# Gate projection of the last block: two products for each k tile instead of three, with a ScalarE copy and a VectorE add

## The chip, the cores and the metric

The kernel runs on one core of one Trainium2 chip. The metric is device time in microseconds (us), the median of several runs. Lower is better.

## The reference

The model is two blocks of mixers with expert layers, and then a last block. Only the last block is touched. For its 256 rows `x` of width 1024 it computes `z = rmsnorm(x) @ w_in`, and splits `z` into `a_in`, `a_gate`, `q`, `k`, `v`, `b_gp` and `g_logits`. The change is in the product that gives three of these:

```
y_a = (multiscale_pool(a_in) * silu(a_gate)) @ w_proj_a
y_b = (dilated_attention(q, k, v) * silu(b_gp)) @ w_proj_b
gates = sigmoid(g_logits + b_gate)            # 2 x 1024 columns
x = x + (gates[0] * y_a + gates[1] * y_b) @ w_out
```

`a_gate` and `b_gp` have 512 columns each and `g_logits` has 2048, so the "gates" stage multiplies 256 rows of width 1024 by 3072 columns. All of it is float32.

## The kernel before

**How a product is made exact enough.** A float32 operand is held as two fp32r parts: a high part (a copy) and a low part (the rest). A product is high by high, plus high by low, plus low by high. The rows are in `XH` and `XL`. They are the two halves of one tile, `X2[:, k, :, :]`, so that 512 adjacent elements are the high and the low part of one k tile of 128. Weights come from HBM in chunks of 128x1024. ScalarE makes `WH` (`high`, L159), then VectorE (`low_v`, L164) or GpSimd (`low_g`, L169, the odd chunks of this stage) makes `WL = raw - WH`. Four slots (`NW`) hold chunks in turn, and `w_used` counts chunks that TensorE has finished.

**The stage.** The gates have 24 chunks. A pair of chunks (`kh` 0 and 1, each with four k tiles) makes two column blocks `j` of 128. The output lies transposed: 128 weight columns on the partitions, 256 rows along the free axis. Weights are the stationary operand, rows are the moving one. `chunk_T` (L190) issues for each k tile and block the three products of `three` (L175 to L178), 256 columns each, into `PS[:, bank, 0:256]`; a chunk has 24. Pairs use banks 0 and 1, then 2 and 3, by turns. After the second chunk of a pair, ScalarE empties bank `j = 0` and VectorE bank `j = 1` (L2119, L2121, L2232, L2234); from pair 8 on ScalarE empties both and applies the sigmoid on the way (L2126). The remaining eight sigmoids run late, from SBUF (L2143).

**What is woven in.** Attention runs in the same loop. After each chunk `c` up to 15, `att2_tensor(t, c + 2)` issues, in this order, the weighted sum of step `i - 2` (L1949, 12 products), the six transposes of step `i - 1` (L1957) and, up to step 15, the scores of step `i` (L1971). Here `i = c + 2`. The scores wait for `b_o`, because they overwrite the banks from which VectorE reads the weighted sum:

```
if i >= 2:
    t.wait_ge(b_o, i - 1)
```

`b_o` is raised in `att2_vector(v, i)` by the scaling of the weighted sum of step `i - 2` (L2171). On VectorE the order within one turn of the loop is: low part of a coming chunk (even `c` only), emptying of the gates (odd `c` only), then `att2_vector(c + 2)`: scaling (L2171), reciprocal (L2176), scores plus bias (L2186), maximum (L2190). On ScalarE it is: high part of a coming chunk (L159), emptying of the gates (odd `c`), then `att2_scalar(c + 2)`: copy of the transposed weights (L2081), exponential (L2085). Each engine runs its instructions in the order written.

**What follows.** After the gates come four chunks of `w_proj_a` (PA) and four of `w_proj_b` (PB), all with `chunk_T` and three products, and then the output projection. On ScalarE the copies of branch b (L2147) stand right behind the last gates. On VectorE the matching subtractions (L2257), the low part of the third PA chunk (L164) and the merge of the first PA chunk (L2274) follow in that order.

`two` (L180 to L183) was there already: the expert layers and their query projection use it. It issues one product of 512 columns (high weights by both parts of the rows) and one of 256 (low weights by the high rows). The expert layers then copy the second half of the bank to `BESIDE` (L1009) on ScalarE and add it on VectorE (L1233).

Of the kernel before, what the change touches and what calls it, by code (L numbers as in the profile page):

```python
# [7 lines left out]
ALU = mybir.AluOpType  # L8
ACT = mybir.ActivationFunctionType
# [8 lines left out]
NW = 4  # L18
# [53 lines left out]
def build(nc, d, out):  # L72
    ctx = ExitStack()
    with ctx:
# [3 lines left out]
        def sem(name):  # L78
            return ctx.enter_context(nc.semaphore(name))
# [3 lines left out]
        XH, XL = X2[:, :, 0, :], X2[:, :, 1, :]  # L83
        raw = sb("raw", [128, NW, SLOT])
        WH = sb("WH", [128, NW, SLOT], F32R)
# [18 lines left out]
        PVT = sb("pvt", [128, PV_N])  # L104
# [66 lines left out]
        def wait_low(e, i):  # L171
            e.wait_ge(w_low_g if low_on_g[i] else w_low_v, low_count[i])
# [7 lines left out]
        def two(t, bank, w, k, first, last):  # L180

            t.matmul(PS[:, bank, :], w[0], X2[:, k, :, :].rearrange("p w t -> p (w t)"), start=first, stop=False)  # L182
            return t.matmul(PS[:, bank, 0:256], w[1], X2[:, k, 0, :], start=False, stop=last)  # L183
# [1656 lines left out]
        def mixer1_gpsimd(g):  # L1840
# [57 lines left out]
        q2_up, k2_up, v2_a, v2_v = sem("q2_up"), sem("k2_up"), sem("v2_by_scalar"), sem("v2_by_vector")  # L1898
        b_mm, b_s, b_mx, b_e, b_T, b_pt, b_r, b_w, b_o = (sem(n) for n in (
            "b_scores", "b_biased", "b_max", "b_exp", "b_turned", "b_pt", "b_inverse", "b_weighed", "b_out"))  # L1900
        gr_a, gr_v, gs_up, sw_up, mx_up, bg_T, bg_up = (sem(n) for n in (
            "gates_by_scalar", "gates_by_vector", "gates_sigmoid", "branches_silu", "branch_a_up", "att_turned2",
            "branch_b_up"))

        y_h, y_l, mg_a, mg_b = sem("merge_high"), sem("merge_low"), sem("merge_a"), sem("merge_b")
# [69 lines left out]
        def block2_tensor(t):  # L1975
# [48 lines left out]
            def gate_bank(pair, j):  # L2024
                if pair < 2:
                    t.wait_ge(v2_v if j else v2_a, 2 + pair)
                elif pair < 10:
                    t.wait_ge(gr_v if j else gr_a, pair - 1)
                else:
                    t.wait_ge(gs_up, 2 * (pair - 10) + j + 1)  # L2030
            for c in range(24):
                pair, kh = divmod(c, 2)
                chunk_T(t, G0 + c, [PS[:, 2 * (pair % 2) + j, 0:256] for j in range(2)], (XH, XL), kh, 8, None,
                        lambda j: gate_bank(pair, j))
                if c < 16:
                    att2_tensor(t, c + 2)
                if c == 17:
                    t.wait_ge(b_o, 16)
                    t.wait_ge(b_pt, 16)
                    for n in range(2):  # L2040
                        for j in range(2):
                            for tt in range(2):
                                m = t.transpose(PS[:, 4 + n, j * 256 + tt * 128:j * 256 + tt * 128 + 128],
                                                ATT[:, tt, (2 * n + j) * 128:(2 * n + j) * 128 + 128], ident)
                        m.then_inc(bg_T, 1)

            def pa_bank(pair, j):
                if pair < 2:
                    t.wait_ge(gs_up, 5 + 2 * pair + j)
                else:  # L2050
                    t.wait_ge(mg_a, 2 * (pair - 2) + j + 1)
            for pair in range(4):
# [22 lines left out]
        def att2_scalar(a, i):  # L2075
# [6 lines left out]
            if i < 16:  # L2082
                s_ = SB[i % 3]
                a.wait_ge(b_mx, i + 1)
                a.activation(s_, s_, ACT.Exp, bias=MXB[:, i:i + 1], accum_out=SUB[:, i:i + 1]).then_inc(b_e, 1)  # L2085

        def block2_scalar(a):
            norm_scalar(a, 4, XS2, lambda t, h: x_after_up(a, 3, t, h))
            split_scalar(a, 4, PV_MIX2)
            for c in range(4):  # L2090
                high(a, A0 + c + 3)
            a.wait_ge(w_used, A0 + 4)
            a.activation(AI[:, 0, :], PS[:, 0, :], ACT.Copy).then_inc(ai_a, 1)
            for c in range(24):
                high(a, QK0 + c + 3)
                if c % 2 and c >= 12:
                    pair = c // 2
                    a.wait_ge(w_used, QK0 + c + 1)
                    for j in range(2):
                        a.activation(KT2[:, 2 * pair + j - 12, :], PS[:, 2 * ((pair + 1) % 2) + j, 0:256],  # L2100
                                     ACT.Copy).then_inc(k2_up, 1)
            for c in range(12):
                high(a, V0 + c + 3)
                if c % 4 == 3:
                    nb = c // 4
                    a.wait_ge(w_used, V0 + c + 1)
                    a.activation(VN[:, 0, nb * 512:nb * 512 + 512], PS[:, 2 * ((nb + 1) % 2), :], ACT.Copy).then_inc(v2_a, 1)
                if c in (8, 9):
                    att2_scalar(a, c - 8)
            for c in range(24):  # L2110
                high(a, G0 + c + 3)
                if c % 2:
                    pair = c // 2
                    blk = 2 * pair
                    a.wait_ge(w_used, G0 + c + 1)
                    if pair < 8:
                        ps = PS[:, 2 * (pair % 2), 0:256]
                        if blk < 8:
                            a.activation((SAG if blk < 4 else BGT)[:, blk % 4, :], ps, ACT.Copy).then_inc(gr_a, 1)  # L2119
                        else:  # L2120
                            a.activation(GT[:, blk - 8, :], ps, ACT.Identity,  # L2121
                                         bias=PVT[:, PV_BG + blk - 8:PV_BG + blk - 7]).then_inc(gr_a, 1)
                    else:
                        for j in range(2):
                            b = blk + j
                            a.activation(GT[:, b - 8, :], PS[:, 2 * (pair % 2) + j, 0:256], ACT.Sigmoid,  # L2126
                                         bias=PVT[:, PV_BG + b - 8:PV_BG + b - 7]).then_inc(gs_up, 1)
                if c < 16:
                    att2_scalar(a, c + 2)
                if c == 16:  # L2130
                    a.wait_ge(gr_a, 4)
                    a.wait_ge(gr_v, 4)
                    a.activation(AR[:, 10240:12288], AR[:, 10240:12288], ACT.Silu).then_inc(sw_up, 1)
                if c == 18:
                    a.wait_ge(mx_up, 1)
                    for n in range(2):
                        a.activation(YH[:, 2 * n:2 * n + 2, :], MIX[:, 2 * n:2 * n + 2, :], ACT.Copy).then_inc(y_h, 1)
                if 18 <= c < 22:
                    for j in range(2):
                        b = 2 * (c - 18) + j  # L2140
                        a.wait_ge(gr_v, 8)
                        a.wait_ge(gr_a, 8)
                        a.activation(GT[:, b, :], GT[:, b, :], ACT.Sigmoid).then_inc(gt_sig, 1)  # L2143
            for n in range(2):
                a.wait_ge(bg_up, n + 1)
                a.wait_ge(w_used, PA0)
                a.activation(XH[:, 4 + 2 * n:6 + 2 * n, :], BGT[:, 2 * n:2 * n + 2, :], ACT.Copy).then_inc(y_h, 1)  # L2147

            def merged(kp):
                a.wait_ge(mg_b, 2 * kp + 2)  # L2150
                a.wait_ge(w_used, PA0 if kp < 2 else W0)
                a.activation(XH[:, 2 * kp:2 * kp + 2, :], MG[:, 2 * kp:2 * kp + 2, :], ACT.Copy).then_inc(y_h, 1)
            for c in range(8):
                high(a, PA0 + c + 3)
                if c in (4, 5):
                    merged(c - 4)
            for kp in (2, 3):
                merged(kp)
            table(a, ACT.Sqrt)
            for c in range(8):  # L2160
                high(a, W0 + c + 3)
            norm_scalar(a, 5, SQ2, lambda t, h: x_after_out(a, 4, t, h))


        def att2_vector(v, i):
# [11 lines left out]
            if i < 16:  # L2177
# [11 lines left out]
                v.wait_ge(b_s, i + 1)  # L2189
                v.tensor_reduce(MXB[:, i:i + 1], s_, AX, ALU.max, negate=True).then_inc(b_mx, 1)  # L2190

        def block2_vector(v):
            norm_vector(v, 4, XS2)
            split_vector(v, 4, PV_MIX2)
# [28 lines left out]
                    att2_vector(v, c - 8)  # L2223
            for c in range(24):
                low_v(v, G0 + c + 2)
                if c % 2 and c < 16:
                    pair = c // 2
                    blk = 2 * pair + 1
                    v.wait_ge(w_used, G0 + c + 1)
                    ps = PS[:, 2 * (pair % 2) + 1, 0:256]  # L2230
                    if blk < 8:
                        v.tensor_copy((SAG if blk < 4 else BGT)[:, blk % 4, :], ps).then_inc(gr_v, 1)  # L2232
                    else:
                        v.tensor_scalar(GT[:, blk - 8, :], ps, PVT[:, PV_BG + blk - 8:PV_BG + blk - 7], None,  # L2234
                                        ALU.add).then_inc(gr_v, 1)
                if c < 16:
                    att2_vector(v, c + 2)
                if c == 16:
# [25 lines left out]
            for c in range(8):  # L2264
                low_v(v, PA0 + c + 2)
                v.wait_ge(w_used, PA0 + c + 1)
                if c == 0:
                    v.wait_ge(gs_up, 8)
                    v.wait_ge(gt_sig, 8)
                for j in range(2):  # L2270
                    blk = 2 * (c % 4) + j
# [176 lines left out]
```

## Time and profile before

| | before |
|---|---|
| median of 3 runs | 2162.6 us (2161.62 to 2164.62) |
| the profiled execution's own time | 2162.53 us |
| its span | 2160.7 us |
| TensorE busy (matmul) | 2125.7 us, 98% |
| VectorE busy | 1460.7 us, 68% |
| ScalarE busy | 1270.8 us, 59% |
| GpSimd busy | 357.8 us, 17% |

The profile gives the start of an instruction in us from the start of the span, and how long it took. The gates stage lies at about 1983 to 2107 us. TensorE is the engine that has least idle time; in a row of the weights' load (PEld) or the product (PE) the engine's next instruction may start before the shown end of the one before, since ends of products are modelled. So distances between starts are the ones to measure with.

### The profile page before, as it was taken

The numbers are of one execution on the slowest core, as the hardware profiler recorded it, in microseconds if no ns is written. First come the engines' busy times: TensorE is split into PE (matmuls) and PEld (weight loads), VectorE is DVE, ScalarE is ACT, GpSimd is POOL, SyncE is SP. The second block draws the span as 40 slices with busy tenths as digits, with TensorE's granted clock in tenths as the row PEclk, the third lists the DMA queues.
The fourth block names the chain that finished last, engine by engine and source line by source line (L and its number), as shares of the span: only waits on it lengthen the run. The fifth ranks groups of instructions, "written<-read, shape, count | busy, mean of one in ns | idle before, by whom it ended". The sixth has DMA issues, their size and how long they took to land.

```text
span 2160.7 us, 32784 instructions
## 1 busy us (share of the span) xinstructions
PE 2125.7 (98%) x12752; PEld 1855.5 (86%) x12752; DVE 1460.7 (68%) x2546; ACT 1270.8 (59%) x2137; POOL 357.8 (17%) x171
## 2 busy tenths in 40 slices
PE   8899999999999999999999999999999999999998
PEld 7789988888888888887899888888888888898997
DVE  7658988889855555557489888898555555423445
ACT  6664588877644444455545888876444444444464
POOL 1437800000000000011378000000000000243131
PEclk9999999999999999999999999999999999999999
DMA  6445655555566666653456555555666666754244
GB/s 220 143 132 166 186 170 164 174 169 170 159 205 195 193 193 191 195 178 113 126 165 184 174 167 168 174 173 163 203 194 194 194 192 192 254 185 147 80 136 127
DMA packets 104893, 373.19 MB, mean 173 GB/s; under 512 B 12140, under 2 KB 15620, under 8 KB 104356
## 3 DMA queue, kind: packets, MB, share of 16 engines
q1 hardware_dynamic: 104740, 371.11, 55.8%
q8 instruction: 101, 1.65, 0.3%
q14 instruction: 52, 0.43, 0.1%
HBM read 369.97 MB, written 1.10 MB: 172 GB/s over the span
## 4 chain that ended last, share of the span: by engine, by line
PE 93%; DVE 3%; ACT 2%; DMA 1%; issue 1%; POOL 0%; SPq 0%; ACTq 0%; POOLq 0%; DVEq 0%
PE ps L182 20%; PE ps L176 18%; PE ps L178 18%; PE ps L177 18%; PE ps L183 10%; PE ps L907 3%; PE ps L1971 1%; PE ps L1949 1%; DMA raw<-in_w_qk_dram 1%; DVE WL L164 1%; PE ps L277 1%; PE ps L886 1%; PE ps L1957 1%; PE ps L1422 0%; PE ps L287 0%
## 5 line engine op out<-in xcount | busy, mean ns | idle before, releaser
L159 ACT ACTIVATE WH<-raw 128x1024 fp32r<-128x1024 f32 x680 | 717.6, 1057 | 506.8 <-PE ps L178 457.1
L164 DVE TENSOR_TENSOR WL<-raw,WH 128x1024 fp32r<-128x1024 f32 x556 | 680.3, 1225 | 104.3 <-ACT WH L159 104.1
L182 PE MATMUL ps<-X,WH 128*128 128x512 f32 x1888 | 669.0, 398 | 0.1
L183 PE MATMUL ps<-X,WL 128*128 128x256 f32 x1888 | 527.8, 280 | 0.0
L169 POOL TENSOR_TENSOR WL<-raw,WH 128x1024 fp32r<-128x1024 f32 x124 | 307.6, 2483 | 1001.5 <-ACT WH L159 1000.6
L182 PEld LDWEIGHTS ps<-X,WH 128*128 128x128 f32 x1888 | 353.9, 187 | 79.1 <-issue 0.5
L176 PE MATMUL ps<-WH,X 128*128 128x512 f32 x960 | 378.3, 394 | 6.7 <-DVE X L1607 3.4
L178 PE MATMUL ps<-WH,X 128*128 128x512 f32 x960 | 374.5, 390 | 0.0
L177 PE MATMUL ps<-WL,X 128*128 128x512 f32 x960 | 374.3, 390 | 0.0
L183 PEld LDWEIGHTS ps<-X,WL 128*128 128x128 f32 x1888 | 356.4, 189 | 0.0
L176 PE MATMUL ps<-X,WH 128*128 128x256 f32 x896 | 256.2, 286 | 1.0 <-DVE WL L164 1.0
L177 PE MATMUL ps<-X,WH 128*128 128x256 f32 x896 | 253.5, 283 | 0.0
L178 PE MATMUL ps<-X,WL 128*128 128x256 f32 x896 | 253.5, 283 | 0.0
L176 PEld LDWEIGHTS ps<-WH,X 128*128 128x128 f32 x960 | 180.7, 188 | 47.1 <-DVE X L1607 4.1
L178 PEld LDWEIGHTS ps<-WH,X 128*128 128x128 f32 x960 | 180.6, 188 | 38.1
L177 PEld LDWEIGHTS ps<-WL,X 128*128 128x128 f32 x960 | 180.8, 188 | 37.1 <-issue 0.5
L176 PEld LDWEIGHTS ps<-X,WH 128*128 128x128 f32 x896 | 171.7, 192 | 6.3 <-issue 2.7
L177 PEld LDWEIGHTS ps<-X,WH 128*128 128x128 f32 x896 | 171.9, 192 | 0.1
L178 PEld LDWEIGHTS ps<-X,WL 128*128 128x128 f32 x896 | 171.8, 192 | 0.0
L991 ACT ACTIVATE ONE<-ONE,GATE 128x128 f16<-128x128 f16 x512 | 167.6, 429 | 0.0
L1252 DVE TENSOR_TENSOR X<-arena,X 128x512 fp32r<-128x512 f32 x84 | 58.1, 692 | 161.9 <-ACT X L1038 161.9
L177 PE MATMUL ps<-WL,GH 128*128 128x512 f32 x352 | 137.0, 389 | 0.0
(300 smaller groups left out, 2356.5 us busy)
## 6 DMA issues: line engine op xcount, KB each, us to landing
raw<-in_l_down_dram SPq DMA_DIRECT2D x256, 512.0 KB, 3.6
raw<-in_l_up_dram SPq DMA_DIRECT2D x256, 512.0 KB, 4.3
raw<-in_l_wq_dram SPq DMA_DIRECT2D x32, 512.0 KB, 3.6
raw<-in_w_qk_dram SPq DMA_DIRECT2D x24, 512.0 KB, 3.8
raw<-in_w_gates_dram SPq DMA_DIRECT2D x24, 512.0 KB, 3.6
raw<-in_l_nat_dram SPq DMA_DIRECT2D x16, 512.0 KB, 3.6
raw<-in_l_wout_dram SPq DMA_DIRECT2D x16, 512.0 KB, 3.6
raw<-in_l_win_dram SPq DMA_DIRECT2D x16, 512.0 KB, 4.1
```

What stands on the lines that cost most here:

```text
L159: a.activation(WH[:, i % NW, :], raw[:, i % NW, :], ACT.Copy).then_inc(w_high, 1)
L164: v.tensor_tensor(WL[:, i % NW, :], raw[:, i % NW, :], WH[:, i % NW, :], ALU.subtract).then_inc(w_low_v, 1)
L169: g.tensor_tensor(WL[:, i % NW, :], raw[:, i % NW, :], WH[:, i % NW, :], ALU.subtract).then_inc(w_low_g, 1)
L176: t.matmul(o, a[0], b[0], start=first, stop=False)
L177: t.matmul(o, a[0], b[1], start=False, stop=False)
L178: return t.matmul(o, a[1], b[0], start=False, stop=last)
L182: t.matmul(PS[:, bank, :], w[0], X2[:, k, :, :].rearrange("p w t -> p (w t)"), start=first, stop=False)
L183: return t.matmul(PS[:, bank, 0:256], w[1], X2[:, k, 0, :], start=False, stop=last)
L277: t.matmul(PS[:, bank, 384:512], ident, ident, start=True, stop=True)
L907: m = t.matmul(PS[:, 6 + j // 4, (j % 4) * 128:(j % 4) * 128 + 128], ONE[:, s % 2, 0, g, :, tt], ROWS[:, s % 2, 1 + k, g, :, tt], start=(k ...
L991: a.activation(ROWS[:, s % 2, 1, g, :, t], ROWS[:, s % 2, 2, g, :, t], ACT.Copy, scale=GATE0[:, 8 * s + j:8 * s + j + 1]).then_inc(row_0, 1)
L1252: v.tensor_tensor(gl, G[:, 2 * p:2 * p + 2, :].rearrange("p e t -> p (e t)"), gh, ALU.subtract).then_inc(g_low, 1)
```

## The change

The 24 gate chunks use `two` in place of `three`: per k tile and block one product of 512 columns and one of 256. The bank then holds two halves that must be added. ScalarE copies the second halves of both banks of a pair to `BESIDE` (128x512 in one instruction), for all twelve pairs. VectorE waits for this copy and adds: one `tensor_tensor` of 128x512 for pairs 0 to 3, and two `scalar_tensor_tensor` of 128x256 with the bias for pairs 4 to 11. ScalarE no longer applies the sigmoid out of PSUM: all sixteen gate blocks get it late, in eight activations of 128x512 from SBUF. The semaphore `gs_up` is gone; `gr_a` now counts copies and `gr_v` pairs.

```diff
             for c in range(24):
                 pair, kh = divmod(c, 2)
-                chunk_T(t, G0 + c, [PS[:, 2 * (pair % 2) + j, 0:256] for j in range(2)], (XH, XL), kh, 8, None,
-                        lambda j: gate_bank(pair, j))
+                wait_low(t, G0 + c)
+                for j in range(2):
+                    if kh == 0:
+                        gate_bank(pair, j)
+                    for kk in range(4):
+                        m = two(t, 2 * (pair % 2) + j,
+                                [v[:, (G0 + c) % NW, kk * 256 + j * 128:kk * 256 + j * 128 + 128] for v in (WH, WL)],
+                                4 * kh + kk, kh + kk == 0, kh == 1 and kk == 3)
+                m.then_inc(w_used, 1)
...
+        def gates_sigmoid(a, n):
+            a.wait_ge(gr_v, 5 + n)
+            a.activation(GT[:, 2 * n:2 * n + 2, :], GT[:, 2 * n:2 * n + 2, :], ACT.Sigmoid).then_inc(gt_sig, 1)
...
                 if c % 2:
                     pair = c // 2
-                    blk = 2 * pair
+                    b = 2 * (pair % 2)
                     a.wait_ge(w_used, G0 + c + 1)
...
+                    if pair >= 2:
+                        a.wait_ge(gr_v, pair - 1)
+                    a.activation(BESIDE[:, pair % 2], PS[:, b:b + 2, 256:512], ACT.Copy).then_inc(gr_a, 1)
+                if c >= 18:
+                    gates_sigmoid(a, c - 18)
...
+            for n in (6, 7):
+                gates_sigmoid(a, n)
...
+        def gates_vector(v, pair):
+
+            blk, b = 2 * pair, 2 * (pair % 2)
+            v.wait_ge(gr_a, pair + 1)
+            if pair < 4:
+                o = (SAG if blk < 4 else BGT)[:, blk % 4:blk % 4 + 2, :]
+                v.tensor_tensor(o, PS[:, b:b + 2, 0:256], BESIDE[:, pair % 2], ALU.add).then_inc(gr_v, 1)
+            else:
+                for j in range(2):
+                    n = blk + j - 8
+                    m = v.scalar_tensor_tensor(out=GT[:, n, :], in0=PS[:, b + j, 0:256], scalar=PVT[:, PV_BG + n:PV_BG + n + 1],
+                                               in1=BESIDE[:, pair % 2, j], op0=ALU.add, op1=ALU.add)
+                m.then_inc(gr_v, 1)
...
-                if c % 2 and c < 16:
...
+                if c % 2:
+                    gates_vector(v, c // 2)
                 if c < 16:
                     att2_vector(v, c + 2)
```

## Rows read from the trace of the kernel before

**Rows 1.** The page: TensorE's busy time (share, count), and the chain that ended last.
```profile
PE 2125.7 (98%) x12752; PEld 1855.5 (86%) x12752; DVE 1460.7 (68%) x2546; ACT 1270.8 (59%) x2137; POOL 357.8 (17%) x171
...
PE 93%; DVE 3%; ACT 2%; DMA 1%; issue 1%; POOL 0%; SPq 0%; ACTq 0%; POOLq 0%; DVEq 0%
```
**Rows 2.** Busy time by stage: PE, PEld, DVE, ACT, POOL, then granted clock, DMA share, GB/s.
```profile
1983.00:2107.00 124.00, 124.00 (x951) 115.39 (x950) 57.30 (x88) 63.35 (x95) 31.45 (x13) 1.00 0.35 108
```
**Rows 3.** TensorE in order of time (start, us, what): gate chunks 16, 17, 48 products between.
```profile
2083.10 0.36 PE L176 MATMUL ps<-X,WH 128*128 128x256 f32 x1
...
2088.94 0.82 PE L2043 MATMUL ps<-cst,arena 128*128 128x128 f32 x6
```
**Rows 4.** TensorE in order of time: two chunk pairs of the query projection, 32 products each.
```profile
153.86 0.47 PE L182 MATMUL ps<-X,WH 128*128 128x512 f32 x1
...
159.50 1.05 PE L886 MATMUL ps<-arena 128*128 128x128 f32 x8
...
166.75 0.48 PE L182 MATMUL ps<-X,WH 128*128 128x512 f32 x1
...
172.49 1.05 PE L886 MATMUL ps<-arena 128*128 128x128 f32 x8
```
**Rows 5.** TensorE in order of time: gate chunk 3 and the attention step behind it.
```profile
2002.39 0.39 PE L176 MATMUL ps<-X,WH 128*128 128x256 f32 x1
...
2005.37 1.45 PE L1949 MATMUL ps<-arena 128*128 128x64 f32 x12
2006.66 0.83 PE L1957 MATMUL ps<-cst,arena 128*128 128x128 f32 x6
2007.42 1.56 PE L1971 MATMUL ps<-arena 64*128 64x256 f32 x6
```
**Rows 6.** ScalarE in order of time, the same turn of the loop.
```profile
2005.41 1.04 ACT L159 ACTIVATE WH<-raw 128x1024 fp32r<-128x1024 f32 x1
2006.36 0.36 ACT L2119 ACTIVATE arena<-ps 128x256 f32<-128x256 f32 x1
```
**Rows 7.** VectorE in order of time, the same turn of the loop.
```profile
2005.57 0.42 DVE L2232 COPY arena<-ps 128x256 f32<-128x256 f32 x1 [1.13 <-PE ps L178]
2006.86 0.28 DVE L2171 TENSOR_SCALAR arena<-ps,sm 128x64 f32<-128x64 f32 x1 [0.86 <-PE ps L1949]
```
**Rows 8.** ScalarE in the first expert layer: the copy of a second half.
```profile
278.11 0.60 ACT L1009 ACTIVATE BESIDE<-ps 128x512 f32<-128x512 f32 x1 [0.50 <-PE ps L183]
```
**Rows 9.** VectorE there: the add behind this copy, and its next instruction.
```profile
278.74 0.69 DVE L1233 TENSOR_TENSOR arena<-ps,BESIDE 128x512 f32<-128x512 f32 x1 [1.08 <-ACT BESIDE L1009]
279.35 0.68 DVE L1219 TENSOR_TENSOR ONE<-ONE,GP 128x1024 f16<-128x1024 f16 x1
```
**Rows 10.** Groups of instructions, VectorE, 1840 to 1870 us (busy us, mean ns | idle before).
```profile
L306 DVE SCALAR_TENSOR_TENSOR X<-ps,pvt,X 128x256 fp32r<-128x256 f32 x8 | 3.2, 476 | 1.7 <-ACT X L298 1.7
```
**Rows 11.** The chain that ended last, in order of time: VectorE releases TensorE.
```profile
1870.20 1.24 DVE WL L164
1871.48 0.38 PE ps L176
```
**Rows 12.** TensorE in order of time: starts of the first and the third PA chunk.
```profile
2107.08 0.28 PE L176 MATMUL ps<-Y,WH 128*128 128x256 f32 x1
...
2112.84 0.28 PE L176 MATMUL ps<-Y,WH 128*128 128x256 f32 x1
```
**Rows 13.** ScalarE behind the last gates.
```profile
2108.01 1.15 ACT L2147 ACTIVATE X<-arena 128x512 fp32r<-128x512 f32 x2
```
**Rows 14.** VectorE behind the last gates.
```profile
2109.88 1.22 DVE L164 TENSOR_TENSOR WL<-raw,WH 128x1024 fp32r<-128x1024 f32 x1
2111.02 0.75 DVE L2274 TENSOR_TENSOR arena<-ps,arena 128x256 f32<-128x256 f32 x2
```
**Rows 15.** VectorE beside GpSimd, in order of time: two views, one row of each.
```profile
2091.91 2.90 DVE L2253 TENSOR_TENSOR Y<-arena,Y 128x512 fp32r<-128x512 f32 x1
...
2091.00 3.26 POOL L169 TENSOR_TENSOR WL<-raw,WH 128x1024 fp32r<-128x1024 f32 x1 [3.98 <-ACT WH L159]
```

More of the change, by code:

```diff
@@ L1900, in build @@
             "b_scores", "b_biased", "b_max", "b_exp", "b_turned", "b_pt", "b_inverse", "b_weighed", "b_out"))
-        gr_a, gr_v, gs_up, sw_up, mx_up, bg_T, bg_up = (sem(n) for n in (
-            "gates_by_scalar", "gates_by_vector", "gates_sigmoid", "branches_silu", "branch_a_up", "att_turned2",
+        gr_a, gr_v, sw_up, mx_up, bg_T, bg_up = (sem(n) for n in (
+            "gates_by_scalar", "gates_by_vector", "branches_silu", "branch_a_up", "att_turned2",
             "branch_b_up"))
@@ L2026, in gate_bank @@
                     t.wait_ge(v2_v if j else v2_a, 2 + pair)
-                elif pair < 10:
-                    t.wait_ge(gr_v if j else gr_a, pair - 1)
                 else:
-                    t.wait_ge(gs_up, 2 * (pair - 10) + j + 1)
+                    t.wait_ge(gr_v, pair - 1)
             for c in range(24):
                 pair, kh = divmod(c, 2)
-                chunk_T(t, G0 + c, [PS[:, 2 * (pair % 2) + j, 0:256] for j in range(2)], (XH, XL), kh, 8, None,
-                        lambda j: gate_bank(pair, j))
+                wait_low(t, G0 + c)
[7 more added lines that the diff above has]
+                m.then_inc(w_used, 1)
                 if c < 16:
@@ L2048, in pa_bank @@
                 if pair < 2:
-                    t.wait_ge(gs_up, 5 + 2 * pair + j)
+                    t.wait_ge(gr_v, 11 + pair)
                 else:
@@ L2113, in block2_scalar @@
                     pair = c // 2
-                    blk = 2 * pair
+                    b = 2 * (pair % 2)
                     a.wait_ge(w_used, G0 + c + 1)
[L2116 to L2127, printed above, removed]
+                    if pair >= 2:
[3 more added lines that the diff above has]
+                    gates_sigmoid(a, c - 18)
                 if c < 16:
@@ L2130, in block2_scalar @@
                 if c == 16:
-                    a.wait_ge(gr_a, 4)
                     a.wait_ge(gr_v, 4)
@@ L2137, in block2_scalar @@
                         a.activation(YH[:, 2 * n:2 * n + 2, :], MIX[:, 2 * n:2 * n + 2, :], ACT.Copy).then_inc(y_h, 1)
[L2138 to L2143, printed above, removed]
+            for n in (6, 7):
+                gates_sigmoid(a, n)
             for n in range(2):
@@ L2225, in block2_vector @@
                 low_v(v, G0 + c + 2)
-                if c % 2 and c < 16:
[L2227 to L2235, printed above, removed]
+                if c % 2:
+                    gates_vector(v, c // 2)
                 if c < 16:
@@ L2267, in block2_vector @@
                 if c == 0:
-                    v.wait_ge(gs_up, 8)
                     v.wait_ge(gt_sig, 8)
```

## The prediction

> **What bounds the kernel now.** I read the page first: TensorE is busy 98% of the span and carries 93% of the chain that ended last [rows 1]. Busy time by stage comes next. Over the gates, 1983 to 2107 us, TensorE is busy all of the 124.00 us at a granted clock of 1.00, while VectorE works 57.30 us and ScalarE 63.35 us [rows 2]. So a product less on TensorE is worth its whole distance between starts, and work added to the other two costs nothing until it makes TensorE wait. The question for each added instruction is therefore which TensorE wait it stands in front of. Within the stage I read the three engines in order of time over one turn of the loop [rows 5 to 7].
>
> **TensorE's gain.** Per k tile and block, three products of 256 columns become one of 512 and one of 256. The columns streamed are the same, 768. What goes is one instruction and one weight load. The two forms can be compared in the trace, with the same operands in the same roles. With three, the 48 products of two chunks take 2088.94 - 2083.10 = 5.84 us [rows 3]. With two, a pair of chunks in the query projection has 32 products; four of the seven full pairs there take 159.50 - 153.86 = 5.64 us and three take 172.49 - 166.75 = 5.74 us [rows 4]. Their mean is 5.68 us, 0.16 less for two chunks. Most gate chunks stand alone between attention steps, which costs 2005.37 - 2002.39 = 2.98 us for one [rows 5], slightly more than half of 5.84. I take 0.09 us per chunk, so 24 x 0.09 = 2.2 us. The bounds are 12 x 0.10 = 1.2 us (all pairs like the slower row) and 12 x 0.20 = 2.4 us (all like the faster). At 24 chunks x 8 x one instruction, 2.2 us are 11 ns for each instruction removed.
>
> The rows put the 48 products at 0.12 us a start [rows 3]. Against this the Trainium skill (TensorE: Matmul & The Clock Gate, section "Wait — 56ns, not 53.3ns?") says that back-to-back warm products start N / 2.4 GHz + about 2.5 ns apart. By that rule 256 columns would be 109 ns, the removed instruction would be worth 2.5 ns, and the whole gain 192 x 2.5 ns = 0.5 us. The trace does not agree for this operand type, since 5.84 us / 48 is 122 ns. I go by the rows.
>
> **The wait that it adds.** The scores of a step (L1971) wait for VectorE's scaling of the weighted sum (L2171), which stands behind the emptying of the gates in VectorE's order. Before, this was harmless. VectorE's copy starts 0.20 us after the chunk, at 2005.57, and it is idle again before the scaling at 2006.86 [rows 7]. That scaling ends at 2007.14, and the scores start at 2007.42, behind the transposes [rows 5].
>
> After the change VectorE must first wait for ScalarE's copy, and ScalarE is late. It runs the exponential and then the high part of a weight chunk, and gets to the gates only at 2006.36 [rows 6], 0.99 us after the chunk's end. This time does not hang on the chunk's end but on what came before it (scores, maximum, exponential), so it stays 2006.36 - 2002.39 = 3.97 us after the chunk's start. I work in that time:
>
> - ScalarE's copy starts at 3.97.
> - VectorE's add starts 278.74 - 278.11 = 0.63 later [rows 8, 9], at 4.60.
> - The next VectorE instruction starts 279.35 - 278.74 = 0.61 behind the add [rows 9]. So the scaling starts at 5.21 and ends 0.28 later [rows 7], at 5.49.
> - VectorE to TensorE takes 1871.48 - (1870.20 + 1.24) = 0.04 [rows 11], so the scores may start at 5.53.
> - Without the wait they would start at (2.98 - 0.09) + (2007.42 - 2005.37) = 2.89 + 2.05 = 4.94 [rows 5].
>
> TensorE waits 0.59, say 0.6 us. With the biased form (pairs 4 and later) VectorE has two instructions in place of the add. Eight of this kind are busy 3.2 us together, 0.40 us each [rows 10], so 0.80 in place of 0.61, and the wait is 0.8 us. The stop happens at odd chunks that are followed by scores, which are c = 1, 3, 5, 7 (add) and 9, 11, 13 (biased). After c = 15 there are no scores. The sum is 4 x 0.6 + 3 x 0.8 = 4.8 us. At even chunks nothing is emptied and nothing changes. The delay doesn't grow from turn to turn, since scores, maximum and exponential all start later with TensorE.
>
> Bounds of the 4.8: if the last products' end and not the high part let ScalarE begin, its copy would start at the chunk's end + 0.20, all would be ready 0.20 + 0.63 + 0.61 + 0.28 + 0.04 = 1.76 after the chunk, ahead of 2.05, and the loss would be 0. From above: let no instruction overlap the end of the one before, which puts the add at 0.69 [rows 9] and the two biased ones at 2 x 0.476 = 0.95 [rows 10], and let the release take 0.20, as from the chunk's end to VectorE's copy [rows 5, 7], in place of 0.04. That adds 4 x 0.24 + 3 x 0.31 = 1.9 us, 6.7 in all. The rows are nearest to the middle, because every link of the sum has one.
>
> **Late gates, sigmoids.** Without attention ScalarE and VectorE have a whole pair (about 5.7 us) to empty two banks, and need 0.63 + 0.80. ScalarE's work falls there: sixteen activations out of PSUM and eight late sigmoids of 256 go, and twelve copies and eight sigmoids of 512 come. I cost it at nothing until the last pair.
>
> Behind the last pair ScalarE before had its two sigmoids and began the branch copies at 2108.01, 0.93 us after the first PA product at 2107.08 [rows 12, 13]. Now it has a copy at 0.20, then three sigmoids. The two branch copies of the same size took 1.15 for two [rows 13], with an end overlap of about 0.08 that leaves some 0.53 each. So the branch copies begin at 0.20 + 0.49 + 3 x 0.53 = 2.28, which is 1.35 us later. VectorE's subtractions, the low part of PA's third chunk and the first merge all move by 1.35. The first of the two merges freed its bank at about 2111.02 + 0.42 = 2111.44, and TensorE needed it at 2112.84 [rows 12, 14]: a slack of 1.4 us. The low part was ready at 2111.10, a slack of 1.7. So the slack is just used up. I take 0.1 us, with bounds 0 and 0.5. Behind it everything is again counted from TensorE.
>
> **The sum.** -2.2 + 4.8 + 0.1 = +2.7 us. The profiled execution's own time is 2162.53 us (span 2160.7 and 1.8 around it), as good as the median of 2162.6. The forecast is 2165.2 us. A difference of 0.2%, 4.3 us, is about what a measurement here can tell from no change; the forecast is inside it, on the slow side.
>
> **Rivals.**
>
> - *The wait never binds (faster).* TensorE gets its 2.2 us and the stops are 0: 2162.5 - 2.2 + 0.1 = 2160.4 us. For it: VectorE has 0.86 us of idle before the scaling [rows 7]. Against it: ScalarE's place in the order. It decides at the start of the copy. If it came before 4.94 - 0.63 - 0.61 - 0.28 - 0.04 = 3.38 us after the chunk's start, there would be no stop; the row has 3.97.
> - *Columns alone set the pace.* Then 768 columns take as long in either form, the gain is 0, and the time is 2162.5 + 4.8 + 0.1 = 2167.4 us. Against it is the comparison of [rows 3, 4], though those lie 1900 us apart. The rule of the Trainium skill named above comes near to this: with 0.5 us of gain it would be 2166.9.
> - *VectorE meets GpSimd behind the last gates.* A VectorE subtraction of two SBUF operands took 2.90 us when GpSimd's was already running [rows 15], against the 0.6 us of its like. If GpSimd's next low part begins ahead of VectorE's, the third PA chunk comes some 2.3 us late: 2167.5 us. For it: VectorE's work moves by 1.35 us. Against it: ScalarE's high part, which releases GpSimd, stands behind the same branch copies and moves with it. The Trainium skill (SBUF — State Buffer, section "Who interferes with whom") calls it an exclusive lock for the whole instruction; the row agrees. The new adds read one operand from PSUM, so they don't take part.
> - *Each stop is longer.* With the upper bound of 6.7 us the time is 2162.5 - 2.2 + 6.7 + 0.1 = 2167.1, and with the smaller gain of 1.2 us 2168.1 us.
>
> **Chances.** Forecast 0.70, no wait 0.10, columns alone 0.06, the meeting with GpSimd 0.06, longer stops 0.08. The first two lie within 0.2% of before, except for a few hundredths at the edges. Of the other three (0.20) most lie past 2166.9. So faster 0.02, same 0.81, slower 0.17. The likeliest case's own range is 2163.5 to 2166.6. The full range reaches 2161.5 (stops half as long, and scatter of the runs) to 2168.0.
>
> **What would show it.** A pair of gate chunks 16 and 17 takes about 5.65 us. Between L1957 and L1971 TensorE waits at seven odd chunks, 0.6 us at four and 0.8 us at three, released by VectorE's L2171 line; at even chunks it doesn't. VectorE's idle before the new adds is released by ScalarE's copy, which starts about 3.97 us after the chunk. A turn of the loop becomes 0.09 us shorter at even chunks and 0.5 to 0.7 us longer at odd ones. The forecast is wrong if these waits are missing, if a chunk is not shorter, or if the third PA chunk starts more than 0.5 us late.

## The result and the profile after

The changed kernel takes 2165.68 us (median of 20 runs, 2164.05 to 2167.69) against 2163.37 us before (20 runs, 2161.34 to 2165.07). The ratio of the two is 1.0013, with a 95% interval of 1.0007 to 1.0019. It is 2.3 us slower by the medians, where +2.7 us was forecast. The interval excludes 1, and the difference is inside the 0.2% that the prediction called no change.

The spans of the two profiled executions differ by only 2162.2 - 2160.7 = 1.5 us. The code ahead of the gates is the same in both, and yet the first gate product starts at 1981.48 us instead of 1982.98. That is scatter of earlier stages, so I compare the distance between two events of one trace: the first gate product and the first product of the next projection (PA). I call it the stage. It was 124.10 us before. Here are the stage and the PA chunks in the changed kernel (columns as in [rows 2]), and then TensorE's waits within the stage (who waited for whom, us in total, times, longest).

```profile
1981.48:2108.39 126.91, 123.00 (x760) 105.16 (x759) 60.22 (x98) 64.13 (x89) 31.25 (x13) 1.00 0.35 105
2108.39:2120.05 11.66, 11.66 (x99) 11.56 (x97) 7.40 (x12) 7.24 (x10) 6.51 (x2) 1.00 0.54 165
```

```profile
PE ps L1971 <- DVE arena L2168: 3.9, 7, 0.7
```

The stage is 2.81 us longer. TensorE, which was busy all of it in [rows 2], now stands idle for 126.91 - 123.00 = 3.9 us. All of that is one wait, seven times: the scores (L1971) for VectorE's scaling (L2168, which was L2171). (A stop costs slightly more than the idle time shown for it, 0.54 us against 0.48 in the turn below, since the shown end of the transposes lies past the point at which the scores would have started.) The granted clock is still 1.00. PA is 0.14 us longer than before, where its row was:

```profile
2107.08:2118.60 11.52, 11.52 (x99) 11.52 (x97) 5.74 (x10) 6.01 (x8) 6.14 (x2) 1.00 0.63 181
```

The three engines in gate chunk 3, the turn of [rows 5 to 7], look like this. First TensorE, in order of time:

```profile
2001.28 0.50 PE L182 MATMUL ps<-X,WH 128*128 128x512 f32 x1
...
2004.21 1.45 PE L1949 MATMUL ps<-arena 128*128 128x64 f32 x12
2005.49 0.82 PE L1957 MATMUL ps<-cst,arena 128*128 128x128 f32 x6
2006.79 1.56 PE L1971 MATMUL ps<-arena 64*128 64x256 f32 x6 [0.48 <-DVE arena L2168]
```

Then ScalarE:

```profile
2004.30 1.04 ACT L159 ACTIVATE WH<-raw 128x1024 fp32r<-128x1024 f32 x1
2005.25 0.57 ACT L2127 ACTIVATE BESIDE<-ps 128x512 f32<-128x512 f32 x1
2006.35 0.81 ACT L2086 ACTIVATE arena<-ps 128x768 f32<-128x768 f32 x1 [0.53 <-PE ps L1957]
```

And VectorE:

```profile
2005.85 0.69 DVE L2195 TENSOR_TENSOR arena<-ps,BESIDE 128x512 f32<-128x512 f32 x1 [2.52 <-ACT BESIDE L2127]
2006.46 0.28 DVE L2168 TENSOR_SCALAR arena<-ps,sm 128x64 f32<-128x64 f32 x1
```

Read them as one chain, counted from the chunk's start at 2001.28. ScalarE runs the high part of a weight chunk until about then, and its copy starts at 3.97. The add starts at 4.57, the scaling at 5.18 and ends at 5.46, and the scores start at 5.51. The transposes would have let them start at 2.93 + 2.04 = 4.97, so the stop is 0.54 us. With the biased form (pairs 4 and later) VectorE does two instructions before the scaling:

```profile
2046.19 0.88 DVE L2199 SCALAR_TENSOR_TENSOR arena<-ps,pvt,BESIDE 128x256 f32<-128x256 f32 x2 [2.52 <-ACT BESIDE L2127]
2046.98 0.28 DVE L2168 TENSOR_SCALAR arena<-ps,sm 128x64 f32<-128x64 f32 x1
```

```profile
2047.31 1.56 PE L1971 MATMUL ps<-arena 64*128 64x256 f32 x6 [0.65 <-DVE arena L2168]
```

Here, in chunk 9, the scaling starts 0.79 us behind the first of them instead of 0.61. The scores start 2.76 us after that chunk's end at 2044.55, against 2.03 to 2.04 at the turns without a stop.

### The profile page after: what moved, and what is told of

The parts are those of the page before. It is cut to its first block, busy times and chain, and to the rows that moved or that the text cites. A ratio compares the mean times of both kernels' runs of the same rounds, so it can differ in the third digit from the quotient of the medians.

```text
span 2162.2 us, 32409 instructions
## 1 busy us (share of the span) xinstructions
PE 2124.5 (98%) x12560; PEld 1845.5 (85%) x12560; DVE 1465.3 (68%) x2558; ACT 1272.5 (59%) x2133; POOL 357.9 (17%) x171
## 4 chain that ended last, share of the span: by engine, by line
PE 92%; DVE 4%; ACT 2%; issue 2%; POOL 0%; DMA 0%; SPq 0%; ACTq 0%; DVEq 0%; POOLq 0%
PE ps L182 22%; PE ps L176 17%; PE ps L178 17%; PE ps L177 17%; PE ps L183 11%; PE ps L907 3%; PE ps L1971 1%; PE ps L277 1%; DVE WL L164 1%; PE ps L886 1%; PE ps L1949 1%; PE ps L287 0%; PE ps L1422 0%; DVE arena L2183 0%; DVE sm L2187 0%
## 5 line engine op out<-in xcount | busy, mean ns | idle before, releaser
L182 PE MATMUL ps<-X,WH 128*128 128x512 f32 x2080 | 739.1, 398 | 0.1
L182 PEld LDWEIGHTS ps<-X,WH 128*128 128x128 f32 x2080 | 390.0, 187 | 91.8 <-issue 5.1
L183 PEld LDWEIGHTS ps<-X,WL 128*128 128x128 f32 x2080 | 392.7, 189 | 0.0
L176 PE MATMUL ps<-X,WH 128*128 128x256 f32 x704 | 200.1, 284 | 0.0
L177 PE MATMUL ps<-X,WH 128*128 128x256 f32 x704 | 199.2, 283 | 0.0
L178 PE MATMUL ps<-WH,GL 128*128 128x512 f32 x352 | 136.9, 389 | 0.0
L176 PE MATMUL ps<-WH,GH 128*128 128x512 f32 x352 | 136.9, 389 | 0.0
L176 PEld LDWEIGHTS ps<-X,WH 128*128 128x128 f32 x704 | 135.1, 192 | 0.2
```

The costliest lines, as they stand in the source:

```text
L176: t.matmul(o, a[0], b[0], start=first, stop=False)
L177: t.matmul(o, a[0], b[1], start=False, stop=False)
L178: return t.matmul(o, a[1], b[0], start=False, stop=last)
```

## The experiments

All times are compared with the kernel before, run on the same chip. For a few tenths of a us the stage in the trace is the sharper measure, since the times of one kernel spread over 3 us or more. By the times alone e1, e2 and e4 are at the edge of no change (their intervals reach 1.0), so what is said of these three rests on the stage.

**e1_scale_first.** Only VectorE's order changes: the scaling goes in front of the add.

```diff
-        def att2_vector(v, i):
+        def att2_vector(v, i, between=None):
...
                 v.reciprocal(SUB[:, n:n + 1], SUB[:, n:n + 1]).then_inc(b_r, 1)
+            if between is not None:
+                gates_vector(v, between)
...
-                if c % 2:
+                if c % 2 and c >= 16:
                     gates_vector(v, c // 2)
                 if c < 16:
-                    att2_vector(v, c + 2)
+                    att2_vector(v, c + 2, c // 2 if c % 2 else None)
```

> The changed kernel with one thing reordered on VectorE: at odd chunks up to 15 the scaling of the weighted sum (and the reciprocal) comes first, then the add of the two gate halves, then scores plus bias and maximum. Work and products are the same. Theory (the scores wait for a scaling that stands behind an add that stands behind a late ScalarE copy): the waits of L1971 on VectorE, 0.53 us at four and 0.72 us at three odd chunks (4.3 us in all), vanish. The stage from the first gate product to the first PA product, 124.10 us before and 126.91 us after, becomes 122.6 us, and the time is about 1.4 us under the kernel before (near 2162.0, ratio 0.9993). Rival A (more VectorE and ScalarE work in the stage slows it wherever it stands): stage near 126.9, ratio 1.0013. Rival B (the add now delays scores plus bias): a new wait before the exponential, each odd turn 0.2 us or more too long, stage 124 to 126.

Measured: 2161.81 us (11 runs), ratio 0.9991 (0.9982 to 1.0). The stage, the same turn on VectorE, and the same on TensorE:

```profile
1981.86:2104.14 122.28, 122.28 (x759) 105.00 (x758) 61.62 (x98) 64.15 (x89) 30.26 (x13) 1.00 0.35 109
```

```profile
2005.51 0.28 DVE L2168 TENSOR_SCALAR arena<-ps,sm 128x64 f32<-128x64 f32 x1 [2.36 <-PE ps L1949]
2005.71 0.15 DVE L2173 RECIPROCAL sm<-sm 128x1 f32<-128x1 f32 x1
2005.78 0.67 DVE L2197 TENSOR_TENSOR arena<-ps,BESIDE 128x512 f32<-128x512 f32 x1
```

```profile
2004.03 1.45 PE L1949 MATMUL ps<-arena 128*128 128x64 f32 x12
2005.31 0.82 PE L1957 MATMUL ps<-cst,arena 128*128 128x128 f32 x6
2006.06 1.56 PE L1971 MATMUL ps<-arena 64*128 64x256 f32 x6
```

The scores start 2.03 us after the chunk, and TensorE is busy for all of the 122.28 us. With the same work on every engine the stage is 4.63 us shorter than in the changed kernel. The seven turns with a stop, each from chunk start to chunk start, account for 49.59 - 45.17 = 4.42 us of this. The other 0.2 us are not stops. The largest part lies in the last six chunks, where TensorE waits in neither kernel; here they are in the changed kernel and then in e1:

```profile
2091.34:2108.39 17.05, 17.05 (x100) 14.81 (x99) 9.69 (x13) 12.15 (x17) 7.91 (x3) 1.00 0.53 170
```

```profile
2087.42:2104.14 16.72, 16.72 (x99) 14.63 (x98) 9.71 (x13) 12.16 (x17) 7.93 (x3) 1.00 0.62 196
```

These 0.33 us are taken up again at the end; in the remaining chunks the difference is 0.1 us the other way.

Rival A (more work slows it wherever it stands) and rival B (the add delays what follows) both fall.

**e2_copy_first.** Only ScalarE's order changes, at odd chunks up to 15; VectorE still scales behind the add.

```diff
-                high(a, G0 + c + 3)
+                if c % 2 == 0 or c >= 16:
+                    high(a, G0 + c + 3)
...
                     a.activation(BESIDE[:, pair % 2], PS[:, b:b + 2, 256:512], ACT.Copy).then_inc(gr_a, 1)
+                    if c < 16:
+                        high(a, G0 + c + 3)
```

> The changed kernel with one thing reordered on ScalarE: at odd chunks up to 15 the copy of the second halves comes ahead of the high part of a weight chunk. VectorE's order is that of the changed kernel. Theory: ScalarE's copy starts 0.20 us after the chunk instead of 1.04, the scaling is done 1.8 to 1.95 us after the chunk and the scores could start at 2.05 anyway, so the stops vanish here too although the scaling still stands behind the add: stage 122.6 us, about 1.4 us under the kernel before. Rival A (the place of the scaling behind the add is what costs, whenever the copy comes): stops stay at 0.5 to 0.7 us, stage 126.9. Rival B (the high part, now 0.5 us later, makes a weight chunk late): a wait of TensorE for a low part, not for L2168.

Measured: 2162.11 us (11 runs), ratio 0.9991 (0.9982 to 1.0). The stage, and then TensorE, ScalarE and VectorE in the same turn:

```profile
1983.34:2105.62 122.28, 122.28 (x759) 105.01 (x758) 60.40 (x98) 64.93 (x89) 30.37 (x13) 1.00 0.36 109
```

```profile
2002.58 0.50 PE L182 MATMUL ps<-X,WH 128*128 128x512 f32 x1
...
2005.51 1.45 PE L1949 MATMUL ps<-arena 128*128 128x64 f32 x12
2006.79 0.82 PE L1957 MATMUL ps<-cst,arena 128*128 128x128 f32 x6
2007.54 1.13 PE L1971 MATMUL ps<-arena 64*128 64x256 f32 x4
```

```profile
2005.70 0.60 ACT L2128 ACTIVATE BESIDE<-ps 128x512 f32<-128x512 f32 x1
2006.20 1.05 ACT L159 ACTIVATE WH<-raw 128x1024 fp32r<-128x1024 f32 x1
```

```profile
2006.34 0.69 DVE L2198 TENSOR_TENSOR arena<-ps,BESIDE 128x512 f32<-128x512 f32 x1 [1.70 <-ACT BESIDE L2128]
2006.99 0.28 DVE L2171 TENSOR_SCALAR arena<-ps,sm 128x64 f32<-128x64 f32 x1
```

The copy starts 0.19 us after the chunk, the scaling is done at 1.76, and the scores start at 2007.54, which is 2.03. So the scaling may stand behind the add, as long as the copy comes in time. It took both to make the stop: a consumer behind the add on VectorE, and the copy behind the high part on ScalarE. Taking away either removes all of it.

**e3_three_products.** The changed kernel with three products of 256 columns, into the two halves of the bank.

```diff
+        def split3(t, bank, w, k, first, last):
+
+            t.matmul(PS[:, bank, 0:256], w[0], X2[:, k, 0, :], start=first, stop=False)
+            t.matmul(PS[:, bank, 256:512], w[0], X2[:, k, 1, :], start=False, stop=False)
+            return t.matmul(PS[:, bank, 0:256], w[1], X2[:, k, 0, :], start=False, stop=last)
...
-                        m = two(t, 2 * (pair % 2) + j,
+                        m = split3(t, 2 * (pair % 2) + j,
```

> The changed kernel with three products of 256 columns again, of which high weights by low rows goes into the second half of the bank; copy, adds, sigmoids and all orders as in the changed kernel. It shows what one instruction less is worth while everything else stays. Theory: even chunks and those from 15 on lengthen by 0.063 us each; at the seven odd chunks with a stop a longer chunk costs nothing, since the copy counts from the chunk's start, so their stops shrink from 0.53 to 0.48 and from 0.72 to 0.67. Stage 126.91 + 17 x 0.063 = 128.0 us, time about 3.9 us over the kernel before (ratio 1.0018). Rival (columns alone set the pace, and the stage gained nothing from fewer products): stage 126.9, as after.

Measured: 2168.21 us (11 runs), ratio 1.0024 (1.0015 to 1.0033). The stage, and TensorE's waits in it:

```profile
1985.48:2113.54 128.06, 124.57 (x951) 115.46 (x950) 60.22 (x98) 64.14 (x89) 31.30 (x13) 1.00 0.34 104
```

```profile
PE ps L1977 <- DVE arena L2174: 3.5, 7, 0.6
```

The stage is 1.15 us longer than in the changed kernel (expected 1.1), and the stops total 3.5 us instead of 3.9. Fewer products do pay, but where there is a stop the shorter chunk only makes the stop longer.

**e4_products_only.** The kernel before with the two products and its own emptying. The half of the bank with high weights by low rows isn't added, so that product is missing from the gates.

```diff
-                chunk_T(t, G0 + c, [PS[:, 2 * (pair % 2) + j, 0:256] for j in range(2)], (XH, XL), kh, 8, None,
-                        lambda j: gate_bank(pair, j))
+                wait_low(t, G0 + c)
+                for j in range(2):
+                    if kh == 0:
+                        gate_bank(pair, j)
+                    for kk in range(4):
+                        m = two(t, 2 * (pair % 2) + j,
...
+                m.then_inc(w_used, 1)
```

> The kernel before with the products of the change alone: one of 512 columns and one of 256 for each k tile, and the emptying of before (0:256 of each bank, ScalarE and VectorE in parallel, sigmoids out of PSUM). The second half of each bank is left out, so the product of high weights and low rows is missing from the gates. Theory: no stop, 24 chunks of 0.063 us less, stage 124.10 - 1.5 = 122.6 us, time 1.5 us under the kernel before (ratio 0.9993). Rival (columns alone): stage 124.1, ratio 1.0. Rival (my sizing before the result, 0.09 us per chunk): stage 121.9.

Measured: 2162.25 us (11 runs), ratio 0.9991 (0.9982 to 1.0).

```profile
1982.56:2104.95 122.39, 122.39 (x760) 105.19 (x759) 57.36 (x88) 63.38 (x95) 31.41 (x13) 1.00 0.36 109
```

The products alone gain 124.10 - 122.39 = 1.71 us, as good as e1's 1.82. So with the order of e1, the copy and the add cost nothing in the stage. The rival of columns alone falls. 1.8 us over 24 chunks are 0.076 us each; expected were 0.063 (from the result) and 0.09 (from the prediction).

**e6_one_add.** The changed kernel, biased pairs with one add as well. It leaves out the bias of the gates.

```diff
-                for j in range(2):
-                    n = blk + j - 8
-                    m = v.scalar_tensor_tensor(out=GT[:, n, :], in0=PS[:, b + j, 0:256], scalar=PVT[:, PV_BG + n:PV_BG + n + 1],
-                                               in1=BESIDE[:, pair % 2, j], op0=ALU.add, op1=ALU.add)
-                m.then_inc(gr_v, 1)
+                v.tensor_tensor(GT[:, blk - 8:blk - 6, :], PS[:, b:b + 2, 0:256], BESIDE[:, pair % 2],
+                                ALU.add).then_inc(gr_v, 1)
```

> The changed kernel, with the two biased instructions of pairs 4 to 11 replaced by one add of 128x512, as in pairs 0 to 3. The bias of the gates is left out. Theory (a stop is the sum of the links copy, add, scaling): the three stops at c = 9, 11, 13 shrink from 0.72 to 0.53 us, which is the 0.19 us between 0.80 and 0.61; the other four stay. Stage 126.91 - 0.57 = 126.3 us, time 0.6 us under the changed kernel, 1.7 over the kernel before (ratio 1.0008). Rival (the longer stops at later pairs come from something else that changes there): stops stay at 0.72, stage 126.9.

Measured: 2166.1 us (10 runs), ratio 1.0012 (1.0003 to 1.0022), which can't be told from the changed kernel. The stage, and the scores behind chunk 11, which starts at 2056.01 and ends at 2058.89:

```profile
1982.33:2108.87 126.54, 122.95 (x759) 105.18 (x758) 59.09 (x91) 64.09 (x89) 30.80 (x13) 1.00 0.35 106
```

```profile
2061.52 0.70 PE L1971 MATMUL ps<-arena 64*128 64x256 f32 x2 [0.52 <-DVE arena L2168]
```

The scores start 5.51 us after the chunk's start, the same as in pair 1 of the changed kernel, so the chain is what I said. The turns of c = 9, 11 and 13, from chunk start to chunk start, fall from 7.19, 7.20 and 7.19 us to 7.00, which is the 0.57 us expected. The stage nevertheless shrinks by only 0.37 us. The missing 0.20 us is in turns without a stop: the chunks c = 6, 12 and 14 take 2.94 us each here and 2.89, 2.88 and 2.88 in the changed kernel. Why they differ wasn't tried. Counted from the chunk's end the stop at c = 11 is 2.63 - 2.04 = 0.59 us and not the 0.53 expected, because this chunk took only 2.88 us; I had treated the chunk as constant.

**e7_branch_first.** The kernel of e1 with the last three sigmoids behind the branch copies.

```diff
-                if c >= 18:
+                if 18 <= c < 23:
                     gates_sigmoid(a, c - 18)
...
-            for n in (6, 7):
-                gates_sigmoid(a, n)
...
+            for n in (5, 6, 7):
+                gates_sigmoid(a, n)
```

> The kernel of e1_scale_first with ScalarE's last three sigmoids behind the two branch copies instead of ahead of them. In the kernel before, PA (first PA product to first PB product) takes 11.52 us; in the changed one 11.66, since the first merge of PA frees its bank 5.7 us after the last gate and TensorE wants it at 5.76. Theory: the branch copies begin 1.6 us earlier, PA is back at 11.52 us, stage of the gates 122.3 as in e1; 0.15 us in all, which the times can't show. Rival (the 0.14 us comes from GpSimd's subtraction beside VectorE's, not from the sigmoids): PA stays at 11.66.

Measured: 2161.73 us (10 runs), ratio 0.9989 (0.998 to 0.9999). PA in e1 and then in e7:

```profile
2104.14:2115.81 11.67, 11.67 (x99) 11.56 (x97) 7.41 (x12) 7.23 (x10) 6.53 (x2) 1.00 0.51 160
```

```profile
2104.90:2116.41 11.51, 11.51 (x99) 11.51 (x98) 6.59 (x12) 7.22 (x10) 5.44 (x2) 1.00 0.63 194
```

PA is back at the 11.5 us of the kernel before, so the 0.14 us of the changed kernel came from the place of the sigmoids. They are lost where the third PA chunk begins: in e1 two starts in a row are 0.21 and 0.19 us apart there instead of 0.12 (2109.77, 2109.98, 2110.17). That chunk needs the bank which the first merge frees, but the profile shows no wait there, so this last link is argued and not shown. VectorE's low part that is slow beside GpSimd starts only at 2110.76, so it isn't the cause. As a time it can't be seen.

**e5_qk_too.** The kernel of e1, with the 24 chunks of the q and k projection changed in the same way. The core of it:

```diff
-                chunk_T(t, QK0 + c, [PS[:, 2 * ((pair + 1) % 2) + j, 0:256] for j in range(2)], (XH, XL), kh, 8, None,
-                        lambda j: qk_bank(pair, j))
...
+                        m = two(t, 2 * ((pair + 1) % 2) + j,
...
+                    a.activation(BESIDE[:, pair % 2], PS[:, b:b + 2, 256:512], ACT.Copy).then_inc(qk_a, 1)
...
+                            v.tensor_tensor(KT2[:, 2 * pair + j - 12, :], ps, be, ALU.add).then_inc(k2_up, 1)
```

> The kernel of e1_scale_first, and the 24 chunks of the q and k projection treated in the same way: one product of 512 and one of 256 columns, ScalarE copies the second halves of a pair, VectorE adds twice 256 (12 pairs). Attention isn't woven into these chunks but for the last, so nothing of TensorE should wait for the adds. Theory: a pair of chunks back to back gains 0.10 to 0.20 us, as in the query projection and at gate chunks 16 and 17, 12 x 0.15 = 1.8 us; time 1.8 us under e1 (near 2160.2, ratio 0.9983 to the kernel before). Rival (the first pairs collide with the pooling work on VectorE, or the last k pair, whose add now follows a copy, delays the v projection or the first scores): ratio 0.999 or more, with a wait of TensorE in that stage.

Measured: 2159.69 us (11 runs), ratio 0.9981 (0.9972 to 0.999). It is faster than both kernels: 4.1 us under the one before in the same series (2163.75). The q and k stage (first product to the first of the v projection) in the kernel before, and then in e5 with its gates stage:

```profile
1871.48:1945.86 74.38, 74.38 (x601) 73.75 (x601) 24.27 (x30) 29.63 (x36) 35.19 (x13) 1.00 0.57 179
```

```profile
1871.31:1943.28 71.97, 71.97 (x409) 62.81 (x408) 26.47 (x39) 33.19 (x38) 40.06 (x13) 1.00 0.59 185
1980.40:2102.69 122.29, 122.29 (x759) 105.00 (x758) 61.62 (x98) 64.13 (x89) 30.25 (x13) 1.00 0.34 109
```

The q and k stage gains 74.38 - 71.97 = 2.41 us, 0.20 a pair, the upper end of what was expected. TensorE doesn't wait in either stage.

## Why the prediction was right

- **Where the loss is.** Named was the wait of the scores for the scaling, at odd chunks 1 to 13 and nowhere else. The trace has exactly seven, at those chunks. e1 and e2 show the two orders that make it, one by one.
- **The chain from the chunk's start.** Forecast 3.97, 4.60, 5.21, 5.49, 5.53 us; measured 3.97, 4.57, 5.18, 5.46, 5.51. All links were read from rows of other stages or of the same turn, and the copy's start was taken from the chunk's start, not from its end. That was the choice that mattered: counted from the end with 0.20 us, the loss would have come out as 0.
- **The size of the stops.** Forecast 4 x 0.6 + 3 x 0.8 = 4.8 us. Measured as starts of L1971 after the chunk's end, less 2.04: 0.56, 0.54, 0.55, 0.54, then 0.72, 0.75, 0.73, which is 4.4; the same seven turns against those of e1 give 4.4 too. The add's and the biased form's 0.61 and 0.80 held (0.61 and 0.79). The stops were rounded up, and chunks with a stop are 0.04 us longer than assumed.
- **TensorE's gain.** Forecast 2.2 us. The changed kernel itself gains 1.6 (its stage less the 4.4 of the stops, 122.5, against 124.1), e1 1.8 and e4 1.7. This term was mis-sized, though it lies within its bounds of 1.2 to 2.4. The faster of the two query rows [rows 4] holds where chunks stand back to back (the q and k stage, 0.20 a pair), but a gate chunk between attention steps is 2.92 to 2.94 us most of the time against 2.98, a gain of 0.05. I had taken 0.09 for both kinds.
- **Behind the gates.** Forecast 0.1 us, measured 0.14, from the place that was named (e7). The links held too: the branch copies begin 2110.66 - 2108.39 = 2.27 us after the first PA product (forecast 2.28), and the first merge moves from 3.94 us behind it to 5.27, by 1.33 (forecast 1.35).
- **The sum.** -1.6 + 4.4 + 0.14 = +2.9 us by the stages; +2.3 by the medians, whose interval (0.07% to 0.19%) is 1.5 to 4.1 us. Forecast +2.7. The gain was forecast 0.6 us too large and the stops 0.4 us too large, and the two errors cancel in good part. That the sum came out this close is partly luck; that the kernel gets slower, and by which wait, is not. In the time itself the forecast was 2165.2 us and the measurement 2165.68, with 2163.37 in place of 2162.5 for the kernel before.
- **The rivals.** The wait that never binds didn't happen, but e2 makes it happen at the point given: its copy starts at 2005.70 - 2002.58 = 3.12 us after the chunk's start, before the limit of 3.38. Columns alone don't set the pace (e3, e4). At 1.7 us for 192 instructions one is worth 9 ns (e4). The Trainium skill (TensorE: Matmul & The Clock Gate, section "Wait — 56ns, not 53.3ns?") gives about 2.5 ns as the fixed cost of a warm back-to-back product; these runs don't agree with it for these operands. Behind the last gates VectorE did not meet GpSimd in the harmful order; one low part took 2.07 us there instead of 1.22, and TensorE didn't wait for it. Longer stops did not occur.

## What to carry to other kernels

Work added to an engine that is half idle costs what stands behind it in that engine's order: look for the next instruction that the bound engine waits for, and count its readiness from the event that really starts the chain (here the exponential and a weight copy, not the end of the product). Put the short instruction that releases the bound engine ahead of the long one that nobody waits for yet; here that turned the stage from +2.8 us into -1.8, and the same product form in a stage without such a neighbour gained 2.4 us at once. And where a difference is 0.1%, measure the stage between two events of the trace, since the stretch ahead of it may move by more than the effect: in these traces the first gate product of kernels that are the same up to there lies anywhere from 1981.48 to 1985.48.

## What the runs showed that I had not expected

A chunk made shorter ahead of such a stop gains nothing. The start of the scores is set by the chain that is counted from the chunk's start, so in these seven turns the gain of the products and a part of the stop cancel: a turn with one add takes 7.00 us from chunk start to chunk start in the changed kernel, and 7.00 in e3, whose chunks are longer (2.98 us) and whose stops are shorter by as much.

And the two-product form has no single pace. The 16 products of a gate chunk between attention steps take 2.92 to 2.93 us in all turns of e1 from the second to the last but one, and 2.86 us in the last one; the changed kernel has 2.88 or 2.89 in some turns. The two chunks 16 and 17, back to back, take 5.63 or 5.64 us, but 5.74 in e4. The last six chunks take 17.05 us in the changed kernel and 17.04 in e6, and 16.72 or 16.73 in e1, e2, e4, e5 and e7, with the same products, no wait of TensorE and a granted clock of 1.00 in all of them. With three products they take 17.35 us in the kernel before and 17.34 in e3, although e3 has stops as well, and a chunk between attention steps is steady at 2.96 to 2.99 from the second on. What sets the pace of the two-product form was not tried and stays open. It is worth up to 0.3 us of a stage, so the stage resolves the 4.4 us of the stops, but not tenths in the value of one product less.
